# A two-layer block in 285 weight blocks: row exponents broadcast by transfers, a second turning bank, reordered VectorE work

## The reference

```
a_cum = cumsum(dt * a)                                   # per head, in each chunk of 128
decay_in = exp(where(causal, a_cum[l] - a_cum[s], -inf))
cb = einsum("bclgn,bcsgn->bcgls", cc, bc)
y_diag = einsum("bcgjls,bcsgjp->bclgjp", cb * decay_in, x_)
states = einsum("bclgn,bcgjl,bclgjp->bcgjpn", bc, exp(a_cum[-1] - a_cum), x_)
prev = scan over chunks: carry * exp(a_cum[-1]) + states
y_off = einsum("bclgn,bcgjpn,bcgjl->bclgjp", cc, prev, exp(a_cum))
y = y_diag + y_off + d_skip * xh
y_s = group_rmsnorm(y * silu(z)) @ w_s_out               # groups of 512 channels
h = h + (sigmoid(gate_a) * y_a + sigmoid(gate_s) * y_s) @ w_o
```

## Time and profile before

| | |
|---|---|
| median of 3 runs | 1872.18 us (1872.11 to 1872.43) |
| profiled execution, its own time | 1872.29 us |
| span from first to last instruction | 1870.5 us |
| granted TensorE clock, mean | 0.989 |
| PE, DVE, ACT busy | 1805.8, 1110.0, 869.4 us |
| PE, DVE, ACT busy from 376 to 462 us, one overlap and what follows it | 81.9, 60.5, 54.1 of 86 us |

### The profile page before, as it was taken

The page is one execution under the profiler, slowest core; times in us unless marked ns, Lnnn a source line. Parts: engine busy times, 40 slices in busy tenths (PEclk is TensorE's granted clock), DMA queues, the critical chain, the costliest instruction groups (busy, mean ns, idle before and its releaser), DMA issues.

```text
span 1870.5 us, 21350 instructions
## 1 busy us (share of the span) xinstructions
PE 1805.8 (97%) x8410; PEld 1466.2 (78%) x8410; DVE 1110.0 (59%) x1601; ACT 869.4 (46%) x1214; POOL 10.0 (1%) x18
## 2 busy tenths in 40 slices
PE   7999999999999899899999998899999999999997
PEld 5888887777767688688888885788888888888885
DVE  6554255767675554565555334476677767668563
ACT  4223235665757522343333223376666666565521
POOL 0000000000000000000000000000000000000000
PEclk9999999999999999999999998999999999999999
DMA  4223222121111122132322331422222212222321
GB/s 174 99 93 102 90 90 79 57 68 57 68 57 68 57 91 101 57 113 92 100 99 93 101 102 67 153 95 80 68 79 80 68 68 79 79 68 80 124 96 73
DMA packets 44674, 162.04 MB, mean 87 GB/s; under 512 B 4896, under 2 KB 5024, under 8 KB 44448
## 3 DMA queue, kind: packets, MB, share of 16 engines
q1 hardware_dynamic: 42560, 153.35, 24.2%
q0 software_dynamic: 2016, 7.34, 1.0%
HBM read 156.48 MB, written 4.19 MB: 86 GB/s over the span
## 4 chain that ended last, share of the span: by engine, by line
PE 83%; DVE 8%; ACT 6%; issue 2%; DMA 0%; DVEq 0%; POOL 0%; ACTq 0%; SPq 0%
PE bank L469 72%; PE bank L677 3%; PE bank L487 2%; ACT w_high L788 2%; DVE Y L1376 1%; ACT L862 1%; DVE seg L1416 1%; PE bank L509 1%; ACT cexp L895 1%; DVE cexp L1421 1%; PE bank L686 1%; PE bank L524 0%; PE bank L606 0%; ACT Y L879 0%; DVE w_low L1259 0%
## 5 line engine op out<-in xcount | busy, mean ns | idle before, releaser
L469 PE MATMUL bank<-u_high,w_high 128*128 128x512 f32 x1656 | 657.6, 397 | 5.7 <-DVE w_low L1259 5.7
L469 PE MATMUL bank<-u_high,w_low 128*128 128x512 f32 x1656 | 645.8, 390 | 0.0
L469 PE MATMUL bank<-u_low,w_high 128*128 128x512 f32 x1656 | 645.7, 390 | 0.0
L1259 DVE TENSOR_TENSOR w_low<-raw,w_high 128x1024 fp32r<-128x1024 f32 x285 | 348.6, 1223 | 332.5 <-ACT w_high L788 324.4
L788 ACT ACTIVATE w_high<-raw 128x1024 fp32r<-128x1024 f32 x285 | 300.5, 1055 | 460.5 <-PE bank L469 444.6
L469 PEld LDWEIGHTS bank<-u_high,w_high 128*128 128x128 f32 x1656 | 311.5, 188 | 74.9 <-issue 13.6
L469 PEld LDWEIGHTS bank<-u_high,w_low 128*128 128x128 f32 x1656 | 311.2, 188 | 66.1
L469 PEld LDWEIGHTS bank<-u_low,w_high 128*128 128x128 f32 x1656 | 311.7, 188 | 62.4 <-issue 1.2
L796 ACT ACTIVATE h_raw<-bank 128x512 f32<-128x512 f32 x44 | 26.3, 597 | 123.8 <-PE bank L469 119.9
L1074 ACT ACTIVATE XL<-XL 128x512 f32<-128x512 f32 x56 | 35.3, 630 | 75.0 <-DVE XL L1638 46.8
L469 PE MATMUL bank<-f_high,w_low 128*128 128x512 f32 x176 | 69.5, 395 | 0.0
(11 more groups left out here) (318 smaller groups left out, 2399.6 us busy)
## 6 DMA issues: line engine op xcount, KB each, us to landing
raw<-stream SPq DMA_DIRECT2D x285, 512.0 KB, 3.2
X<-x_t SPq DMA_DIRECT2D x4, 512.0 KB, 6.5
residual<-X POOLq DMA_DIRECT2D x4, 512.0 KB, 8.5
X<-residual POOLq DMA_DIRECT2D x4, 512.0 KB, 5.8
out_t<-X POOLq DMA_DIRECT2D x4, 512.0 KB, 3.3
masks_f<-masks SPq DMA_DIRECT2D x1, 1280.0 KB, 13.0
ws_t<-spatial_w POOLq DMA_DIRECT2D x1, 512.0 KB, 6.4
bs_row<-spatial_b POOLq DMA_DIRECT2D x1, 512.0 KB, 6.9
```

Source lines behind the costliest of these rows:

```text
L469: ins = pe.matmul(acc[:], w[:, k], x[:, at + k], start=start and k == first and j == 0, stop=stop and k == KT - 1 and j == 2)
L1259: tt(w_low[:, n % RAW_RING], raw[:, n % RAW_RING], w_high[:, n % HI_RING].bitcast(F32), ALU.subtract).then_inc(lo_done, 1)
```

## The change

1. `seg_rows` and the two-part copy of `acum` go. POOL stores `acum` once to DRAM, and loads row n, with a step of 0 between partitions, into one of four SBUF tiles `rows_of`; a tile is loaded again when ACT's `cexp` and DVE's differences of the head four before are done. ACT and DVE read the tile in place of the bank, and the differences no longer wait for `cexp`.
2. The bank that this frees (`side[0]`) takes every second use of the order `THIRD`.
3. DVE's step is put into four turns: the product with C·B first; then `low`, convolution, C·B, turned tiles, states; then differences and the product with C; then outputs, squares and norms.
4. At the end of the zone three tiles of Y are rounded and split before the last head's output is taken, and the casts, the last group's norm and the splits of the second half stand ahead of the `ahead` of the second block of `S_OUT`.
5. `residual` adds the previous square before it waits for its block.
6. The result goes out from SP in eight transfers.

```diff
-        acum_high = fixed("acum_high", [HEADS, T], F32R)
-        acum_low = fixed("acum_low", [HEADS, T], F32R)
+        rows_of = [place(f"rows{k}", [P, T], F32, at) for k, at in enumerate((acum_at, acum_at + 2 * K, F + 112 * K, F + 114 * K))]
...
+        def third_bank(use):
+            return side[3 * (THIRD[use] % 2)]
+        def wait_third(eng, use):
+            eng.wait_ge(s3_done, THIRD[use] + 1)
+            wait_for(eng, s3_free, THIRD[use])
...
+            for k in range(KT):
+                sp.wait_ge(s_fin, k + 1)
+                sp.dma_start(out.rearrange("(k p) t -> p k t", p=P)[:, k:k + 1], X2[:, k:k + 1]).then_inc(s_out, 16)
...
             def third(use):
-                wait_for(pe, s3_free, THIRD[use])
-                return side[3]
+                wait_for(pe, s3_free, THIRD[use] - 1)
+                return third_bank(use)
...
-            def seg_rows(g, h):
-                n = 8 * g + h
-                wait_for(pe, s_exp, 2 * n - 2)
-                for k, part in enumerate((acum_high, acum_low)):
-                    ins = pe.matmul(side[h % 2][:], identR[0:HEADS, n:n + 1].to_broadcast([HEADS, P]), part[:],
-                                    start=k == 0, stop=k == 1)
-                ins.then_inc(s_seg, 1)
...
-                act.wait_ge(s_seg, n + 1)
+                act.wait_ge(s_row[n % 4], 16 * (n // 4) + 16)
                 wait_for(act, s_y, n - 1)
-                act.activation(cexp[:, h % 2], side[h % 2][:], ACT.Exp).then_inc(s_exp, 1)
+                act.activation(cexp[:, h % 2], rows_of[n % 4][:], ACT.Exp).then_inc(s_exp, 1)
...
+            group_square(GROUPS - 1, 2)
+            for k in range(3):
+                cast_y(k)
             for m, key in enumerate(S_OUT):
-                ahead(key)
...
                 if m == 1:
                     for k in range(8, 12):
                         cast_y(k)
                     group_root(GROUPS - 1)
                     for k in range(12, 16):
                         cast_y(k)
+                ahead(key)
...
-                dve.wait_ge(s_exp, 2 * n + 1)
+                dve.wait_ge(s_row[n % 4], 16 * (n // 4) + 16)
...
             for n, key in enumerate(SSD_ZONE):
-                ahead(key)
-                for g in range(GROUPS):
-                    beside(g, n - TEN * g)
+                for turn in range(4):
+                    if turn == 1:
+                        ahead(key)
+                    for g in range(GROUPS):
+                        beside(g, n - TEN * g, turn)
...
+            add_square(last, 2)
+            wait_block(dve, ("gate_s", KT - 1))
+            for k in range(3):
+                split_y(k)
+            take_y(last, 3)
...
+                if j >= 2:
+                    k = j - 1
+                    dve.wait_ge(n_sq, KT // 2 + n * KT + k + 1)
+                    for total, s in ((sums, sq), (sums_b, sq_b))[:2 if both else 1]:
+                        ins = tt(total[:], s[:, 0] if k == 1 else total[:], s[:, k % 2], ALU.add)
...
                 wait_block(dve, key)
                 give(tt(x[:, j], x[:, j], bank(key)[:], ALU.add), key)
                 wait_taken(dve, key)
                 dve.sem_inc(x_added, 1)
...
+            pool.wait_ge(d_acum, 1)
+            pool.dma_start(running, dtw[:, 1]).then_inc(s_rows, 16)
+            pool.wait_ge(s_rows, 16)
+            for n in range(HEADS):
+                if n >= 4:
+                    pool.wait_ge(s_exp, 2 * (n - 4) + 1)
+                    pool.wait_ge(s_min, n - 4 + 1)
+                row = running[n:n + 1, :]
+                pool.dma_start(rows_of[n % 4][:], bass.AP(row.tensor, row.offset, [[0, P], [1, T]])).then_inc(s_row[n % 4], 16)
```

More of the change, by code:

```diff
@@ L381, in build @@
             sem(f"ssd_{k}") for k in "third third_free state state_taken scaled".split())
-        s_seg, s_min, s_exp, s_mat, s_y, s_ytaken = (sem(f"ssd_{k}") for k in "seg min exp mat y ytaken".split())
+        s_min, s_exp, s_mat, s_y, s_ytaken = (sem(f"ssd_{k}") for k in "min exp mat y ytaken".split())
+        s_rows, s_row = sem("ssd_rows"), [sem(f"ssd_row{k}") for k in range(4)]
         z_done, y_gated, g_sq, g_sum, g_root = (sem(k) for k in "z_done y_gated g_sq g_sum g_root".split())
@@ L906, in group_root @@
                 roots_table()
-                act.wait_ge(s3_done, THIRD[("stat", g)] + 1)
-                act.activation(gsum[:, g], side[3][:], ACT.Ln, scale=1.0 / (D_INNER // GROUPS),
+                wait_third(act, ("stat", g))
+                act.activation(gsum[:, g], third_bank(("stat", g))[:], ACT.Ln, scale=1.0 / (D_INNER // GROUPS),
                                bias=eps[:, 0:1]).then_inc(s3_free, 1)
@@ L958, in cast_y @@
                 if k == 0:
+                    act.wait_ge(s3_done, THIRD[("cb", GROUPS - 1)] + 1)
+                    act.wait_ge(s_y, HEADS - 8)
+                if k == 3:
                     act.wait_ge(s_y, HEADS)
                 act.activation(y_high[:, k], Y[:, k], ACT.Copy).then_inc(y_cast, 1)
+            group_square(GROUPS - 1, 2)
+            for k in range(3):
+                cast_y(k)
             for m, key in enumerate(S_OUT):
-                ahead(key)
[L964 to L972, removed]
                 if m == 1:
@@ L978, in _ @@
                         cast_y(k)
+                ahead(key)
+                if m == 0:
+                    for k in range(3, 5):
+                        cast_y(k)
+                    group_square(GROUPS - 1, 3)
+                    for k in range(5, 8):
+                        cast_y(k)
+                    evac(("gate_s", KT - 1), sig_s[:, KT - 1], ACT.Sigmoid)
+                    table[0] = "sigmoid"
             for j in range(KT):
@@ L1474, in _, with beside @@
-            for n, key in enumerate(SSD_ZONE):
-                ahead(key)
-                for g in range(GROUPS):
-                    beside(g, n - TEN * g)
+            def beside(g, i, turn):
+                if turn == 0:
+                    if 10 <= i <= 17:
+                        into_cb(g, i - 10)
+                if turn == 1:
+                    if 1 <= i <= 6:
+                        conv(g, i - 1)
+                    if i == 4:
+                        wait_third(dve, ("cb", g))
+                        tt(CBm[g % 2][:], third_bank(("cb", g))[:].rearrange("p (c t) -> p c t", c=NCH),
+                           cst[:, 2:3].to_broadcast([P, NCH, P]), ALU.mult).then_inc(s3_free, 1)
+                        dve.wait_ge(s3_free, THIRD[("cb", g)] + 1)
+                    if 5 <= i <= 8:
+                        take_x(g, i - 5)
+                    if i == 9:
+                        states(g)
+                if turn == 2:
+                    if 9 <= i <= 16:
+                        differences(g, i - 9)
+                        into_c(g, i - 9)
+                if turn == 3:
+                    if i in TAKE:
+                        take_y(g, TAKE[i])
+                    if i - 1 in TAKE and TAKE[i - 1]:
+                        add_square(g, TAKE[i - 1])
+                    rows = {27: (0, 1), 28: (2, 3)} if g < 2 else {22: (0,), 23: (1,), 25: (2,), 26: (3,)}
+                    for k in rows.get(i, ()):
+                        norm_row(4 * g + k)
@@ L1504, in _ @@
                     dve.wait_ge(y_split, 2 * KT)
+                ahead(key)
+                if m == 0:
+                    for k in range(3, 5):
+                        split_y(k)
+                    add_square(last, 3)
+                    for k in range(5, 8):
+                        split_y(k)
                 if key[2] == 0 or key[1] == 0:
```

95 lines of the change are left out of this document (25 added, 70 removed).

## The result

| | before | after |
|---|---|---|
| median of 4 runs | 1872.31 us (1872.11 to 1874.01) | 1819.84 us (1818.69 to 1821.93) |
| profiled execution, its own time | 1872.29 us | 1818.69 us |
| span | 1870.5 us | 1816.8 us |
| mean granted clock | 0.989 | 0.991 |

The ratio is 0.9719, with a 95% interval of 0.9702 to 0.9736. The change takes off 52.5 us by the medians and 53.7 us by the two profiled spans; 47.2 us were forecast.

A forecast was written before the change was run, and what follows sets the result against it. The prediction took PE to bound the kernel (busy 1805.8 of 1870.5 us). Zone 31.8, output product's start 8.0, norms 5.6 and end 1.8 sum to 47.2 us off 1872.29: 1825.0 us, range 1819 to 1837.

The forecast's parts named there:

- Rows no longer made on PE: State-space zone: taking the row matmul pairs off PE saves 22.2 us, bounds 21.1 and 32.
- a pair that stands alone: Row pair between two blocks, once in each of 4 groups (i = 9): 1.0 us saved; the other 28 give 0.65 each.
- The second bank and the waits: Zone: PE's waits for turned-tile scaling (9.5 us) and the C·B product (1.6) go; 11.1 us, bounds 0 and 11.1.
- DVE and ACT late next: Overlap steps: the loop through DVE and ACT falls behind PE but has spare; 1.5 us charged, bounds 0 and 20.
- rival (a): The loop of DVE and ACT binds PE in the three overlaps: 1843 us, chance 0.12.
- The start of the output product: From the last head into the output product: idle or low-clock time goes, 8.0 us saved, bounds 5 and 8.4.
- The sign that was given: PE takes 23 to 24 us from the last head to the output product's fifth block, at clock 1.00.
- The cost feared for the second half: Output product's start: rounding for the fourth block follows late, behind the second half's work; up to 1 us lost.
- Rival (b): The output product's start, or the end, gives only its lower bound: 1830 us, chance 0.06.
- The norms: PE's product with the partial sums moves ahead at three residuals: 1.1, 3.4 and 1.1 us, sum 5.6, bounds 4 and 6.
- The end: Last output transfer from SP, half the bytes and no POOL preparation: 1.8 us saved, bounds 0 and 2.6.
- Rival (c): Row transfers take over 29 us, so every four heads wait; 1953 us with 45 us transfers, chance 0.02.

The follow-up runs named there:

- experiment 5: Kernel after, with two 32x512 matmuls beside each head put back on PE, their result unread: 1841.71 us, ratio 0.9835.
- experiment 1: Kernel before with only the rows by transfer (part 1), one bank and DVE's old order: 1848.06 us, ratio 0.9863.
- experiment 3: Kernel after with all uses of the third bank in one bank again, DVE's new order kept: 1820.36 us, ratio 0.9714.
- experiment 2: Kernel before with only DVE's new order (part 3), rows still made on PE, one bank: 1860.74 us, ratio 0.9933.
- experiment 4: Kernel after with DVE's old order in the state-space zone, two banks and rows by transfer kept: 1823.86 us, ratio 0.9734.
- experiment 7: Kernel after with the old order of casts, splits and weight rounding at the start of the output product: 1831.23 us, ratio 0.9772.
- experiment 8: Kernel after with the old residual order, partial sums added and multiplied on PE behind the block: 1821.36 us, ratio 0.9730.
- experiment 9: Kernel after with the result written by POOL in four transfers of 512 KB again: 1824.15 us, ratio 0.9743.
- experiment 6: Kernel after with one row tile instead of four, so a row loads only after the head before was read: 1819.25 us, ratio 0.9709.

## Why the prediction was right, and where it was off

The direction and most of the size came true, but the time stayed in the range by 0.8 us only. It lies below the sum of all upper ends (1820), since one term went past its bound.

- **Rows no longer made on PE, 22.2.** Right: 21.9 by time and 22.3 in place (experiment 5), and 22.4 in experiment 1. The 1.0 us taken for a pair that stands alone held 0.15 for a slower border that no run shows; it is 0.87, but two pairs of each group cost that, not one, and the errors nearly cancel.
- **The second bank and the waits, 11.1.** The size is right, the cause was not. The prediction gave 9.5 us to the second bank. With the bank left out 0.7 us return (experiment 3), and the order alone takes all the waits away with one bank (experiment 2). A tile waited because DVE came to the one before it late, 9.1 us after its start, behind a convolution of 2.31 and the work of a head; moving that scaling ahead of the differences makes it 5.2 and takes the wait away. That the size came out right is luck: the gain was booked to the wrong part. The new order is the part that bears this term. The bank could have helped some without it: 2.4 us, by the sum in experiment 4.
- **DVE and ACT late next, 1.5 charged.** The loop is real (8.89 us against 7.35 of PE in the two longest steps), but costs nothing; the estimate of 9.4 was 0.5 too long, 0.27 of it the differences, which take 0.86 for four from a tile in SBUF and 1.13 from a bank. With the old order it does cost 4.2 us (experiment 4), so rival (a) was held off by part 3. The 1.5 not spent is most of the difference between 33.8 us for the zone and the 31.8 forecast; the other 0.5 is not assigned.
- **The start of the output product, 8.0, bounds 5 and 8.4.** This is the step that failed, by 4.5 us and past its bound. The mechanism was right, the stretch was misread. I took 658.75 for the start of the fifth block and charged four whole blocks (22.8 us) to the 31.25. It is the start of the matmul that follows 78 of the 96, and the fifth block starts at 662.87. The right sum is 78 x 0.227 and one group sum of 0.95, 18.7, and 31.25 - 18.7 = 12.6, near what came (12.5 here, 12.4 in experiment 7). The sign that was given, 23 to 24 us to the fifth block, was right (23.0): only the start of the fifth block in the kernel before was misread. The check was in the row itself: 22.60 us of busy PE at a clock of 0.89 can't hold 22.8 us of work that needs the full clock. The cost feared for the second half (up to 1 us) did not come. Rival (b) was on the wrong side.
- **The norms, 5.6.** 5.4 between the profiles, but part of it is luck of the clock: 3.4 us of it rest on one row at the lower level, and undoing the step gives 1.5 by time and 3.5 in place (experiment 8).
- **The end, 1.8, bounds 0 and 2.6.** It gave 3.0. 256 KB from SP land after 2.1 us; the forecast had SP's 3.2 for 512 KB as its nearest row. The Trainium skill, page "DMA: Bandwidth & Descriptors", section "Anatomy of one DMA — SWDGE (gpsimd) path", would have 2.6 for them, an estimate by that page, whose sum is for GpSimd's path; the measured 2.1 is below, and it is measured for SP's queue. What I left out is POOL's closing of its queue, named in the prediction but given no price: 1.2 us before and 3.9 in experiment 9.
- **Rival (c), late row transfers.** 6.1 us at the most against 29, and even one tile instead of four costs nothing (experiment 6). The reading of the earlier trace rows was wrong in one point: DVE's last scaling ended at 1865.09, so the last transfer was not prepared beside a busy DVE. The three before it were, and all four took 0.71 to 0.72 us.
- **-1.05 at the program start** is not from the change: it lies before any changed work on the path. Ten other profiles with the same code up to there have the first block's start between 18.94 and 20.41 us; before has 18.96 and after 19.64, which is 0.68 of the 1.05; the rest comes within the next 4 us.

## What to carry to other kernels

When an engine waits for a buffer, look at what the releasing engine did before it released: putting that release ahead in its list may take the whole wait away (11.6 us here); a second buffer beside it adds 0.7. When a stretch with an idle gap and a low clock is priced, count its matmuls from the trace and multiply by the pitch at full clock; the border of a block guessed from a time costs more than any other error here (4.5 us). And where the bottleneck engine is given less work, price the loop through the helpers with its lead, not by its length: six steps of 50.3 us in all, against the 46.2 estimated for PE, cost nothing here.

## What the runs showed of the hardware

- A pair of 32x512 matmuls between blocks costs 0.70 us of PE's time on average (experiment 5); its matmuls are listed with 0.50 and 0.39.
- The same four differences of 128x128 take 0.86 us from SBUF and 1.13 from PSUM, by the rows of step 16. The groups (count | busy us, mean ns | idle before) of the kernel before and of the kernel after:

```profile
L1416 DVE TENSOR_SCALAR seg<-bank,tok 128x128 f32<-128x128 f32 x128 | 36.0, 344 | 23.1 <-ACT cexp L895 22.9
```

```profile
L1423 DVE TENSOR_SCALAR seg<-rows,tok 128x128 f32<-128x128 f32 x128 | 27.8, 280 | 0.2
```

- A row of 2 KB spread to 128 partitions, 256 KB in all, from POOL lands in 3.3 to 6.1 us; 256 KB from SP to DRAM in 2.1.
- Behind the same idle time of 2.22 us, the same products ran once at half rate (2.07 us for two) and once at full rate (1.13). The stretches at the lower level lie differently from run to run, and one profile's row at a norm is good to about 1 us.
